# The last scatter of a mixture-of-experts block started on the running sum, and its evacuation shared between two engines

## The reference, cut to what matters

```python
def grouped_moe(x, w_router, router_bias, w_gate, w_up, w_down):
    ...                                   # group by top-2 sum, top 2 of its experts, gates normalised
    y = jnp.zeros_like(x)
    for e in range(N_EXPERTS):            # 16 experts, D_EXPERT = 1024
        h = jax.nn.silu(x @ w_gate[e]) * (x @ w_up[e])
        y = y + combine[..., e:e + 1] * (h @ w_down[e])
    return y

def reference(...):
    ...                                   # mixer: h_l = h_l + mod_l[2] * out_l
    m_l = modulate(rmsnorm(h_l, norm_ffn_g[layer]), mod_l[3], mod_l[4])
    h_l = h_l + mod_l[5] * grouped_moe(m_l, w_router, router_bias, w_gate[layer], w_up[layer], w_down[layer])
    return h_l                            # (1, 256, 2048)
```

## Time and profile before

| | |
|---|---|
| median of 3 runs | 1445.53 us (1442.14 to 1451.47) |
| the profiled execution | 1452.63 us |
| its span, first to last instruction | 1450.8 us |
| TensorE matmul busy | 1297.9 us (89%) |
| VectorE, ScalarE, GpSimd busy | 427.2, 206.9, 74.9 us |
| DMA | 559.57 MB, mean 386 GB/s |

### The profile page before, as it was taken

How to read it: one execution, slowest core, us unless ns; L and a number is a source line. 1 busy time by engine, 2 the same in 40 slices (tenths; PEclk the granted TensorE clock), 3 DMA queues, 4 the chain that set the end, 5 groups by cost and what they waited for, 6 DMA issues and landing times.

```text
span 1450.8 us, 20436 instructions
## 1 busy us (share of the span) xinstructions
PE 1297.9 (89%) x8678; PEld 619.2 (43%) x8679; DVE 427.2 (29%) x804; ACT 206.9 (14%) x482; POOL 74.9 (5%) x138
## 2 busy tenths in 40 slices
PE   3999999999999996999999999998887877888757
PEld 1656544555454464433632543442432442343223
DVE  2122596777566430202111201121111111111102
ACT  3100101244101142100200110110110110011001
POOL 0012100121132000000000000000000000000000
PEclk9999999999999998999999999999999999999988
DMA  9899868766898899999999999999999999999995
GB/s 392 367 419 389 325 258 329 299 231 240 320 375 344 347 409 394 428 426 385 428 427 419 413 425 428 403 427 427 430 429 428 429 428 428 428 429 428 428 426 243
DMA packets 57019, 559.57 MB, mean 386 GB/s; under 512 B 6640, under 2 KB 6768, under 8 KB 19952
## 3 DMA queue, kind: packets, MB, share of 16 engines
q1 hardware_dynamic: 42048, 502.25, 83.1%
q0 software_dynamic: 14320, 52.01, 9.6%
q10 hardware_dynamic: 576, 4.19, 0.7%
HBM read 556.34 MB, written 2.10 MB: 385 GB/s over the span
## 4 chain that ended last, share of the span: by engine, by line
PE 59%; DMA 33%; DVE 3%; issue 2%; ACT 1%; DVEq 0%; POOL 0%; SPq 0%; ACTq 0%; POOLq 0%
DMA ring<-w_gate_dram 11%; DMA ring<-w_up_dram 11%; PE ps L890 9%; PE ps L599 9%; PE ps L895 9%; PE ps L857 5%; PE ps L914 5%; DMA big<-w_up_dram 4%; DMA ring<-w_half_dram 3%; PE ps L920 3%; PE ps L593 3%; PE ps L711 2%; PE ps L604 2%; DMA ring<-w_in_dram 2%; DMA big<-w_gate_dram 2%
## 5 line engine op out<-in xcount | busy, mean ns | idle before, releaser
L1619 DVE TENSOR_TENSOR big<-ps,big 128x1024 f32<-128x1024 f32 x60 | 70.7, 1219 | 313.3 <-PE ps L843 168.3
L895 PE MATMUL ps<-ring,big 128*64 128x512 f32 x560 | 132.9, 608 | 21.7 <-DMA ring<-w_up_dram 10.6
L599 PE MATMUL ps<-ring,big 128*128 128x512 f32 x320 | 146.9, 601 | 2.5 <-DMA ring<-w_in_dram 2.5
L1254 DVE SCALAR_TENSOR_TENSOR once<-ring,silu_c,once 128x1024 f32<-128x1024 f32 x96 | 123.2, 1283 | 69.8 <-DMA ring<-w_half_dram 64.5
L857 PEld LDWEIGHTS ps<-probs,big 128*128 128x128 f32 x1024 | 119.5, 192 | 44.2 <-issue 37.5
L857 PE MATMUL ps<-probs,big 128*128 128x96 f32 x1024 | 130.0, 280 | 1.9 <-DVE probs L1623 1.9
L890 PE MATMUL ps<-ring,early 128*32 128x256 f32 x1408 | 91.4, 407 | 37.0 <-DMA ring<-w_up_dram 18.3
L711 PE MATMUL ps<-ring,big 128*128 128x512 f32 x240 | 105.0, 593 | 0.0
L599 PEld LDWEIGHTS ps<-ring,big 128*128 128x128 f32 x320 | 59.2, 192 | 72.2 <-issue 66.9
L895 PEld LDWEIGHTS ps<-ring,big 128*64 128x64 f32 x560 | 36.2, 137 | 104.2 <-issue 66.9
L890 PEld LDWEIGHTS ps<-ring,early 128*32 128x32 f32 x1408 | 44.5, 115 | 84.3 <-issue 27.5
(11 more groups left out here) (315 smaller groups left out, 1128.9 us busy)
## 6 DMA issues: line engine op xcount, KB each, us to landing
ring<-w_down_dram SPq DMA_DIRECT2D x48, 2048.0 KB, 22.2
ring<-w_up_dram SPq DMA_DIRECT2D x46, 2048.0 KB, 22.2
ring<-w_gate_dram SPq DMA_DIRECT2D x33, 2048.0 KB, 19.8
ring<-w_half_dram POOLq DMA_DIRECT2D x96, 512.0 KB, 6.8
big<-w_up_dram SPq DMA_DIRECT2D x18, 2048.0 KB, 19.6
ring<-w_mix_dram SPq DMA_DIRECT2D x32, 1024.0 KB, 11.3
late<-w_down_dram SPq DMA_DIRECT2D x16, 2048.0 KB, 22.4
big<-w_gate_dram SPq DMA_DIRECT2D x15, 2048.0 KB, 22.1
```

Source lines behind the costliest of these rows:

```text
L599: mm = pe.matmul(ps[:, b + t, :], nT[:, k, t * P:(t + 1) * P], w, start=(k == 0), stop=(k == KT - 1))
L895: mm = pe.matmul(out_b[1][REST * f:REST * (f + 1), :], rows[1][:, k, :], w[:, kk, f * N:(f + 1) * N], start=(k == 0), stop=(k == KT - 1))
L1254: stt(total, half_slots[:, m % HALF_SLOTS, :], silu_c[:, m % KT, 0:1], total, ALU.mult, ALU.add) \
L1619: tt(y, Yb[:, 2 * h:2 * h + 2, :].rearrange("p a n -> p (a n)"), y, ALU.add).then_inc(summed, 1)
```

## The change

Four things. (1) On TensorE, four matmuls of the identity with tile 0 of `total` write the running sum into `Yb`; the last scatter of tile 0 then accumulates onto it (`start=False`). They wait for `xg_ready` and for VectorE's adds of the job before (`summed`), not for the last job's result. (2) ScalarE copies the two halves of tile 0 out of `Yb` to `total`; VectorE adds the three pieces of tile 1 as it did. (3) The order of the output pieces is tile 0 first half, tile 1 first half, tile 0 second half, then the two quarters of tile 1, with one semaphore for each tile. (4) The register load of `few` stands ahead of the loop over the rest.

```diff
-OUT_PIECES = [(0, 0, 1024), (0, 1024, 2048), (1, 0, 1024), (1, 1024, 1536), (1, 1536, 2048)]
+OUT_PIECES = [(0, 0, 1024), (1, 0, 1024), (0, 1024, 2048), (1, 1024, 1536), (1, 1536, 2048)]
...
             for q, (t, a, b) in enumerate(OUT_PIECES):
-                sp.wait_ge(out_ready, q + 1)
+                sp.wait_ge(out_ready[t], [piece[0] for piece in OUT_PIECES[:q + 1]].count(t))
...
-            def scatter(j, t, banks=Yb, parts=(0, 1)):
+            def scatter(j, t, banks=Yb, parts=(0, 1), start=True):
...
                     mm = pe.matmul(banks[:, q, :], spread_T[0][BASE * q:BASE * (q + 1), t, :],
-                                   outs[0][BASE * q:BASE * (q + 1), :], start=True, stop=True)
+                                   outs[0][BASE * q:BASE * (q + 1), :], start=start, stop=True,
+                                   skip_group_check=not start)
...
             jobs = pe.value_load(n_i[0:1, NUMBERS:NUMBERS + 1], min_val=2, max_val=JOBS - 1)
+            few = pe.value_load(n_i[0:1, bass.ds(jobs + (JOBS - 1), 1)], min_val=0, max_val=1)
             with pe.If(rest):
                 with loop(pairs * 2 + 1, jobs) as j:
                     any_job(j, False)
-            few = pe.value_load(n_i[0:1, bass.ds(jobs + (JOBS - 1), 1)], min_val=0, max_val=1)
             pe.wait_ge(xg_ready, jobs)
+            pe.wait_ge(summed, jobs * 4)
+            for q in range(4):
+                pe.matmul(Yb[:, q, :], ident, total[:, 0, q * N:(q + 1) * N], start=True, stop=True)
             with pe.If(few):
-                scatter(jobs, 0, parts=(0,))
+                scatter(jobs, 0, parts=(0,), start=False)
                 scatter(jobs, 1, ps[:, 0:4, :], parts=(0,))
             with pe.Else():
-                scatter(jobs, 0)
+                scatter(jobs, 0, start=False)
                 scatter(jobs, 1, ps[:, 0:4, :])
...
+            for h in range(2):          # ScalarE
+                act.wait_ge(scattered, jobs * 4 + (h + 1))
+                copy(total[:, 0, h * 1024:(h + 1) * 1024], Yb[:, 2 * h:2 * h + 2, :].rearrange("p a n -> p (a n)")) \
+                    .then_inc(out_ready[0], 1)
...
             for t, a, b in OUT_PIECES:  # VectorE
+                if t == 0:
+                    continue
                 dve.wait_ge(scattered, jobs * 4 + (2 * t + a // 1024 + 1))
-                banks = ps[:, 0:4, :] if t else Yb
-                tt(total[:, t, a:b], banks[:, a // N:b // N, :].rearrange("p a n -> p (a n)"), total[:, t, a:b],
-                   ALU.add).then_inc(out_ready, 1)
+                tt(total[:, t, a:b], ps[:, a // N:b // N, :].rearrange("p a n -> p (a n)"), total[:, t, a:b],
+                   ALU.add).then_inc(out_ready[t], 1)
```

More of the change, by code:

```diff
@@ L354, in build @@
         outs_saved = [sem("outs0_saved"), sem("outs1_saved")]
-        out_ready, out_sent = sem("out_ready"), sem("out_sent")
+        out_ready, out_sent = [sem(f"out{t}_ready") for t in range(TT)], sem("out_sent")
         dve_step, spread_saved = sem("dve_step"), sem("spread_saved")
```

## The result

Over 22 runs of each the changed kernel took 1452.09 us in the median, the kernel before 1449.47 us; the ratio is 1.0024, with a 95% interval of 1.0013 to 1.0035. One run of the kernel before, 1477.38 us, fell into a slow state and is left out of the ratio. By the ratio the change is 3.5 us slower (1.9 to 5.1; the two medians alone differ by 2.6), inside the 1% that I called no change, and clear of 1 by the interval. The profiled execution has a span of 1452.6 us against 1450.8.

The account below looks back on a forecast made before the run. Weight transfers were taken to bound the kernel, so only the tail could change. Identity matmuls 1438.9 to 1442.3, scatter 1.14 us, copy 1.02 us put the first piece 1.3 us later: 1445.5 + 1.3 = 1446.8 us, range 1441.5 to 1453.

Parts of the forecast that it names:

- Bound and size: Whole kernel: weight transfers bound it, only the tail of 13.4 us can change, and no case reaches 1%.
- likeliest case: Tail: identity matmuls start between 1437.9 and 1439.9 at full clock, +0.3 to +2.3 us; chance 0.45.
- half-clock rival: Tail: TensorE's idle still brings half clock, now under the identity matmuls too, +3.0 to +5.6 us; chance 0.28.
- Start of the identity matmuls: Behind the last down-projection matmul: 1.52 us for the way out of the loop, so a start at 1438.9.
- The load: The flag's register load, moved ahead of the loop: with the branch 1.0 us of the 2.53 us gap, free there.
- Identity matmuls: TensorE in the tail: eight records of 0.43 us, 3.4 us at full clock, ahead of the scatter.
- The clock: TensorE in the tail: full clock, since the idle is 1.5 us in place of 2.5; a close call.
- Evacuation: Behind tile 0's scatter (1.14 us): ScalarE copies take 1.02 us each, VectorE beside it; first piece 1.3 us later.
- rival of one after another: Tail: ScalarE and VectorE read PSUM in turn, five evacuations take 4.6 us, +1.7 us; chance 0.10.
- The output's block: End of the tail: output transfers stay one block of 5.4 us behind the first piece; the other pieces keep up.
- The sum: Tail, net of all terms: +1.3 us, by the first output piece being ready at 1444.5 in place of 1443.24.

Follow-up runs that it names:

- e1: The kernel before with only the register load of the last job's flag moved ahead of the rest loop; ratio 0.9992 to the kernel before.
- e4: The kernel before with the early flag load and four identity matmuls, whose result the last scatter overwrites; VectorE adds all pieces; ratio 1.0026 to the kernel before.
- e3: The changed kernel without the four identity matmuls, so tile 0 of the output lacks the running sum; ratio 0.9995 to the kernel before.
- e2: The changed kernel with the flag's register load back behind the loop, ahead of the identity matmuls; ratio 1.0026 to the kernel before.
- e6: As e5, but the last job gathers nothing for a job behind it; ratio 1.0004 to the kernel before.
- e9: The kernel before with the last scatters inside the rest loop, under a condition for the last job; ratio 0.9994 to the kernel before.
- e10: The changed kernel with identity matmuls and last scatters inside the rest loop, under a condition for the last job; ratio 1.0019 to the kernel before.
- e5: The kernel before with the last job's code written out again behind the rest loop, last scatters at each copy's end; ratio 1.0011 to the kernel before.
- e7: As e6, with identity matmuls between the last down-projection matmuls and the changed kernel's evacuation and piece order; ratio 1.0005 to the kernel before.
- e8: As e7, with seven output pieces in place of five, the first ones of 512 columns; ratio 1.0007 to the kernel before.
- e11: As e10, with the last job's gathers replaced by the identity matmuls under the same condition; ratio 1.0007 to the kernel before.

## Why the prediction was right, and where it was off

**Bound and size.** Right: the result lies within 1%, and e1 to e4 put what changed into the tail. The direction, slower by a few microseconds, held for the likeliest case. That the range holds the measured time owes something to luck. I forecast 1446.8 us, and 1452.09 was measured, 5.3 us more. Of these, 3.9 us are the base: the three runs of the kernel before that I had gave 1445.53 us, 22 give 1449.47. The likeliest case by itself (+0.3 to +2.3 on that base) does not reach 1452; the room that I left for half clock and for the runs' spread does. And +3.5 us is the number of the half-clock rival (+3.0 to +5.6), whose mechanism the trace of the changed kernel rules out for its execution. My remark that 1% is about what a measurement of this kernel can tell was far off: over 22 runs the interval is 0.1% either way.

**Start of the identity matmuls.** Forecast 1.52 us behind the last matmul, by a stop elsewhere in the job; measured 2.11 us. The term was 0.6 us too small, and it was not a constant: 3.2 us from the code packet to the first matmul, less what still runs, which gave 1.4 to 2.2 us of idle. The stop that I took it from is no constant either: in the middle of the last job's first 32 matmuls it is 1.52 us in the kernel before, 1.48 in the changed kernel, 2.7 in e1, e3 and e4, and none in e2. I also wrote that 0.77 us of the identity matmuls would be covered by VectorE's scaling. With a start at 1438.9 nothing is: the scaling was over before them, in the forecast as in the run (1437.79 against 1439.14). The sum did not use it. The rule of the Trainium skill (Runtime: NRT & Kernel Launch, Instruction fetch mechanics) that a taken branch out of the current window of code forces a fetch, weighed as a reason to be up to 1.0 us more pessimistic, pointed the right way. The idle was 0.6 us longer than the 1.52 us of the forecast.

**The load.** I left 1.0 us of the gap to the register load and the branch. The load is 0.3 (e2 against the changed kernel) to 1.0 us (the kernel before against e1). Ahead of the loop nothing shows it as a cost: in the changed kernel, e1, e3 and e4 TensorE stops in the last job's first matmuls and then still waits 1.3 to 3.0 us for weights.

**Identity matmuls.** 3.4 us forecast, 3.62 us measured, 3.5 us by the tails of e4 and e1. My 0.43 us for a record left out 0.2 us between the last of them and the scatter.

**The clock.** Full, as forecast, though the idle was 2.1 us and not 1.5. My reason was thin: in the kernel before it fell after an idle of 2.0 us up to there, here it did not after 2.11 us, nor in e2 and e3 after 2.21 us. That this term came out right was luck.

**Evacuation.** The scatter of tile 0 took 1.18 us (1.14 forecast), ScalarE's copy 1.01 us (1.02), and the two engines ran side by side: VectorE's add began 0.86 us after ScalarE's first copy, while the second was to come. The rival of one after another is out, by this overlap and by e3.

**The output's block.** I moved it as a whole, 5.4 us. It grew to 6.0 us, and to over 7 us in other versions: a term that I had taken for constant is not. Nor did the pieces quite keep up: I took SyncE's issues for 0.35 us each, and the last two took 0.95 and 1.19 us, so that the last piece, ready at 1447.21, was issued at 1447.93.

**The sum.** +1.3 us forecast, +2.1 us in the tails of the two profiles: about 0.6 of the difference from the start, 0.2 from the identity matmuls, 0.1 from the transfers (0.5 longer) and what follows them (0.4 shorter). The runs say +3.5 us (1.9 to 5.1). A likely part of what is left is the base that I summed against: in the profiled execution of the kernel before the last scatter ran at half clock, which cost it 0.9 us before the first piece and which only e6 showed besides, whose down projection waits for transfers. If its usual execution has full clock, its tail is 12.5 us and not 13.4, and the other tails stand 0.9 us worse against it. These come nearer to the runs:

| | tail, us | against 12.5 | by the runs |
|---|---|---|---|
| changed | 15.6 | +3.1 | +3.5 |
| e1 | 11.5 | -1.0 | -1.2 |
| e2 | 16.0 | +3.5 | +3.8 |
| e3 | 12.0 | -0.5 | -0.7 |
| e4 | 15.0 | +2.5 | +3.8 |
| e9 | 12.5 | 0.0 | -0.9 |
| e10 | 15.1 | +2.6 | +2.8 |

This is argued from one execution of each, not shown: against 13.4 us these tails too lie within the intervals of their runs, e4's at the very edge. And it doesn't fit the versions outside the table. By the runs e5, e7, e8 and e11 are 0.7 to 1.6 us above the kernel before, while their tails of 11.2 to 12.1 us are 0.4 to 1.3 us below 12.5; they have the stop at the last job's start, or a different last job, but that this is the reason isn't shown either. What makes up the rest of the 3.5 us stays open.

## What to carry to other kernels

Adding in PSUM with an identity matmul is free only where TensorE has time of its own: an fp32 tile of 128x2048 costs 3.6 us, more than the two adds of 1.2 us on VectorE that it replaces, and at the end of this kernel it stood ahead of everything that was left. Before filling a gap on an engine's timeline, ask what the gap is: here it was a jump out of a loop, which delays the filling just as it delayed the work behind it. And a second copy of code to avoid a stop can have its own stop, 9.7 us here: look for it where the new branch is taken, and then ask what the engine would have waited for there anyway. In the one trace of it the 9.7 us made TensorE some 0.6 us later than in the kernel before, which waits for weights there.

## What the runs showed of the hardware that I had not expected

Code fetches compete with data. With a 16 KB packet of the instruction queue inside it a 2 MB output took about 1 us longer (5.5 to 5.9 us with none, 6.8 to 7.1 us with one, 7.3 to 7.7 us with two), and one or two DMA engines finished alone. Holding TensorE back so that it fetched nothing under the output gave 1 us of it back (7.3 to 6.3 us).

From the start of such a packet to the first matmul behind the loop it took 3.16 to 3.22 us in four kernels, however the idle looked, and 3.5 and 4.2 us with a register load behind the jump.
